# Attention's query-key products for two heads at once, on the two halves of the array's rows

## What is computed

```
# branch A, window_attention: 8 heads, 2 groups of keys (A_KV = 2), 4 heads to a group, head width 64
qg = q.reshape(B, N, Q, A_KV, A_GROUP, HEAD_DIM)
s = jnp.einsum('bnqkgd,bnskd->bnkgqs', qg, k, preferred_element_type=jnp.float32) * ATTN_SCALE
...
s = jnp.where(valid[:, None, None], s + bias, -jnp.inf)
m = jnp.maximum(jnp.max(s, axis=-1, keepdims=True), sk)
e = jnp.exp(s - m)
pr = e / (jnp.sum(e, axis=-1, keepdims=True) + jnp.exp(sk - m))
o = jnp.einsum('bnkgqs,bnskd->bnqkgd', pr.astype(v.dtype), v)
# branch B, dsa_attention: the same with keys chosen by top-k of the indexer's scores, no sink
```

## Time and profile before

| | us |
|---|---|
| runs (3) | 1043.62, 1047.68, 1048.21 |
| median | 1047.68 |
| span of the profiled execution | 1044.9 |

### The profile page before, as it was taken

The page is one execution under the profiler, slowest core; times in us unless marked ns, Lnnn a source line. Parts: engine busy times, 40 slices in busy tenths (PEclk is TensorE's granted clock), DMA queues, the critical chain, the costliest instruction groups (busy, mean ns, idle before and its releaser), DMA issues.

```text
span 1044.9 us, 14060 instructions
## 1 busy us (share of the span) xinstructions
PE 930.3 (89%) x5627; PEld 599.2 (57%) x5630; DVE 394.1 (38%) x1071; ACT 260.4 (25%) x529; POOL 123.1 (12%) x133
## 2 busy tenths in 40 slices
PE   7989998998999999998999977887987887887996
PEld 7869995456999998994333322332322222224885
DVE  4179998878242436453111101101101101101885
ACT  6254326675232323222000000000000000001541
POOL 2404730002030000001111111011010011000000
PEclk9999999999999999997999999999999999999998
DMA  8850602001925225356999999999999999996501
GB/s 262 115 153 2 201 2 61 1 1 30 299 62 158 65 61 241 127 206 249 430 425 425 426 429 427 424 429 424 427 426 427 425 427 428 425 428 250 211 26 60
DMA packets 60131, 263.71 MB, mean 252 GB/s; under 512 B 11054, under 2 KB 36030, under 8 KB 46224
## 3 DMA queue, kind: packets, MB, share of 16 engines
q1 hardware_dynamic: 54160, 250.99, 62.5%
q0 software_dynamic: 5296, 9.79, 2.6%
q10 hardware_dynamic: 624, 2.23, 0.6%
HBM read 253.99 MB, written 16.85 MB: 259 GB/s over the span
## 4 chain that ended last, share of the span: by engine, by line
PE 52%; DMA 30%; DVE 13%; ACT 2%; issue 2%; SPq 0%; DVEq 0%; ACTq 0%
DMA arena<-in_w_up 29%; PE ps L1083 13%; PE ps L1250 11%; PE ps L1115 4%; PE ps L1381 4%; DVE nrm L1901 4%; DVE hT L1905 3%; PE ps L871 3%; PE ps L1275 3%; PE ps L1365 2%; PE ps L1000 1%; PE ps L1049 1%; PE ps L1124 1%; PE ps L1028 1%; DVE xf L1905 1%
## 5 line engine op out<-in xcount | busy, mean ns | idle before, releaser
L1250 PE MATMUL ps<-arena,hT 128*64 128x512 f32 x992 | 243.7, 645 | 41.2 <-DMA arena<-in_w_up 41.0
L1250 PEld LDWEIGHTS ps<-arena,hT 128*64 128x64 f32 x992 | 74.5, 141 | 207.6 <-issue 157.5
L2185 DVE TENSOR_TENSOR xf<-xf,ps 128x256 f32<-128x256 f32 x32 | 13.5, 421 | 404.4 <-ACT xf L1666 379.0
L1083 PE MATMUL ps<-arena_merge,arena_merge 128*128 128x256 f32 x624 | 99.7, 287 | 0.0
L1275 PE MATMUL ps<-arena,xf 128*64 128x512 f32 x336 | 76.7, 598 | 12.8 <-DVE xf L2188 12.8
L1083 PEld LDWEIGHTS ps<-arena_merge,arena_merge 128*128 128x128 f32 x624 | 87.4, 188 | 0.0
L826 POOL DMA_INDIRECT expert_rows<-xf,arena x32 | 31.9, 998 | 427.0 <-ACT xf L1670 399.6
L1083 PE MATMUL ps<-xf_merge,arena_merge 128*128 128x256 f32 x480 | 82.0, 288 | 0.0
L1666 ACT ACTIVATE xf<-ps 128x256 f32<-128x256 f32 x30 | 11.5, 384 | 259.0 <-PE ps L1250 259.0
L1083 PEld LDWEIGHTS ps<-xf_merge,arena_merge 128*128 128x128 f32 x480 | 69.3, 188 | 0.0
L1670 ACT ACTIVATE xf<-ps 128x512 f32<-128x512 f32 x30 | 17.9, 597 | 159.8 <-PE ps L1275 159.8
(11 more groups left out here) (300 smaller groups left out, 1317.6 us busy)
## 6 DMA issues: line engine op xcount, KB each, us to landing
arena<-in_w_gate SPq DMA_DIRECT2D x30, 2048.0 KB, 30.0
arena<-in_w_up SPq DMA_DIRECT2D x30, 2048.0 KB, 37.5
arena<-in_w_down SPq DMA_DIRECT2D x11, 2048.0 KB, 37.3
hT<-in_w_down SPq DMA_DIRECT2D x11, 2048.0 KB, 36.5
arena<-in_w_down SPq DMA_DIRECT2D x20, 1024.0 KB, 31.5
arena<-in_w_in SPq DMA_DIRECT2D x10, 1024.0 KB, 6.4
arena<-in_w_in SPq DMA_DIRECT2D x3, 2048.0 KB, 9.9
arena<-in_w_gate SPq DMA_DIRECT2D x8, 512.0 KB, 10.2
```

The lines of the kernel that those rows point to most:

```text
L1083: mm = pe.matmul(w[:, 2 * lo_t:lo_t + hi_t], rounded(st[:, c, cols]), rounded(mv[:, c, lo_t:hi_t]), start=c == 0 and k == 0, stop=c == pla ...
L1250: mm = pe.matmul(ps[g * BLK:(g + 1) * BLK, 2 + s, :], xsT[:, c, col:col + BLK], expert_columns(k, slice(0, 2), c, g), start=c == 0, stop=c ...
```

## The change

The scores of two units of a block are now issued together, by `scores_of_two(u)` at even u. The matmul of each reads only the 64 partitions of its own group, for the queries as for the keys: one lies on the upper half of the array's rows, the other on the lower half, and they write different PSUM banks. The halves of the query planes that no matmul reads any more are not zeroed, and the semaphore that said so (`q_clean`) is gone. The wait for `max_ready` covers both banks before the first of the two.

```diff
-        pool.wait_ge(sw_split, 10)
-        for q, dst in (('qb', qb), ('qa', qx)):
-            for m in range(4):
-                pool.wait_ge(wide_full, WIDE[(q, m)].fill)
-                for h in (2 * m, 2 * m + 1):
-                    lo = (1 - h // HG) * HD
-                    link(pool.memset(dst[lo:lo + HD, plane(h), :], 0.0))
-        pool.sem_inc(q_clean, 1)
...
-        def scores(u):
+        def scores_of_two(u):
+
             br, b, j = UNITS[u]
-            if banks_before(u) is not None:
-                pe.wait_ge(max_ready, banks_before(u) + 1)
+            for v in (u, u + 1):
+                if banks_before(v) is not None:
+                    pe.wait_ge(max_ready, banks_before(v) + 1)
             if u == 0:
                 pe.wait_ge(toep_ready, 1)
-                pe.wait_ge(q_clean, 1)
...
+            two = [scores_at(u), scores_at(u + 1)]
+            last = [None, None]
             for lo in range(0, n, 512):
                 hi = min(n, lo + 512)
-                if b == 's':
-                    for hh in range(HG):
-                        mm = pe.matmul(w[32 * hh:32 * hh + NS, lo:hi], q[:, 2 * hh + j, NP:NT], kT[:, NP + lo:NP + hi],
-                                       start=True, stop=br == 'a')
-                else:
-                    k0 = P * (b + 1) - n
-                    mm = pe.matmul(w[:, lo:hi], q[:, j, tok(b)], kT[:, k0 + lo:k0 + hi], start=True, stop=br == 'a')
...
+                for hh in range(HG if b == 's' else 1):
+                    for g in range(KV):
+                        d = slice(g * HD, (g + 1) * HD)
+                        if b == 's':
+                            last[g] = pe.matmul(two[g][32 * hh:32 * hh + NS, lo:hi], q[d, 2 * hh + g, NP:NT],
+                                                kT[d, NP + lo:NP + hi], start=True, stop=br == 'a')
+                        else:
+                            k0 = P * (b + 1) - n
+                            last[g] = pe.matmul(two[g][:, lo:hi], q[d, j + g, tok(b)], kT[d, k0 + lo:k0 + hi],
+                                                start=True, stop=br == 'a')
+
+            for g in range(KV):
+                if br == 'b':
+                    m0, _ = MSK[b]
+                    for lo in range(0, n, 512):
+                        hi = min(n, lo + 512)
+                        last[g] = pe.matmul(two[g][:, lo:hi], identb[:, :], msk[:, m0 + lo:m0 + hi], start=False, stop=True)
+                last[g].then_inc(s_full, 1)
...
-        for u in range(AHEAD):
-            scores(u)
+        scores_of_two(0)
         for u in range(len(UNITS) + 3):
-            if u + AHEAD < len(UNITS):
-                scores(u + AHEAD)
+            if u % 2 == 0 and u + AHEAD < len(UNITS):
+                scores_of_two(u + AHEAD)
```

More of the change, by code:

```diff
@@ L487, in _program @@
     consts_ready = sem("consts_ready")
-    q_high, ik_high, q_clean = sem("q_high"), sem("ik_high"), sem("q_clean")
+    q_high, ik_high = sem("q_high"), sem("ik_high")
     f_high, f_split, sw_high, sw_split = (sem(n) for n in ["f_high", "f_split", "sw_high", "sw_split"])
@@ L987, in scores @@
             if br == 'b' and j == 0:
                 pe.wait_ge(masks_ready, [0, 1, 2, 3, 's'].index(b) + 1)
-            w = scores_at(u)
             n = unit_keys(br, b)
             q, kT = (qx, kaT) if br == 'a' else (qb, kbT)
+            two = [scores_at(u), scores_at(u + 1)]
+            last = [None, None]
             for lo in range(0, n, 512):
                 hi = min(n, lo + 512)
-                if b == 's':
-                    for hh in range(HG):
-                        mm = pe.matmul(w[32 * hh:32 * hh + NS, lo:hi], q[:, 2 * hh + j, NP:NT], kT[:, NP + lo:NP + hi],
-                                       start=True, stop=br == 'a')
-                else:
-                    k0 = P * (b + 1) - n
-                    mm = pe.matmul(w[:, lo:hi], q[:, j, tok(b)], kT[:, k0 + lo:k0 + hi], start=True, stop=br == 'a')
```

## The result

The change makes the kernel slower: 1049.95 us in the median of 20 runs (1043.88 to 1053.41) against 1045.05 of 20 runs of the kernel before. The ratio is 1.003, with a 95% interval of 1.0016 to 1.0043. The quotient of the two medians would be 1.0047, a little outside it; the medians of this kernel jump by some us with a few runs, and I go by the ratio. In medians that is +4.9 us where I forecast -3.0, by the ratio some +3. The time is inside my range and inside 0.5%, but the change has the other sign.

The account below looks back on a forecast made before the run. No engine is full in attention; its chain of waits sets the time, and everything behind shifts with it. Places in attention sum to -3.0 us, taking the median 1047.68 to 1044.7 us, range 1040.0 to 1050.5.

Parts of the forecast that it names:

- The sum of the places: Seven stretches of attention, estimated one by one for shorter scores, added switches and the new order: -3.0 us in all.
- The two places between 196 and 220 us: Branch a's last and b's first units (196.0 to 204.6), -1.0 us; weighing to transposes (213.4 to 219.9), -0.8 us.
- b, block 1: Branch b's block 1: three weighings on the chain, two thirds of 3 x 0.43 us saved: -0.8 us.
- b, block 0: Branch b's block 0, 128 keys: +0.2 us ahead of the weighing, -0.2 behind it: 0.
- a, blocks 1 to 3: Branch a's blocks 1 to 3: each weighing saves 0.43 us behind it, costs up to 0.35 ahead: -0.6 us.
- b's sample block: Branch b's units 50 and 51: the pair waits for row_max of unit 49 instead of 47, chain end unchanged: 0.
- the memsets at 0: Start of attention: q_clean never held PE, so removing memsets and wait is worth 0; first score within 0.2 us of 162.5.
- The clock falls: Rival in attention: two more half-clock stretches, net 0 to +0.4 us; over 0.5% slower only at four or more; chance 0.08.
- the sign of being wrong: End of attention, forecast near 254.2 us: the prediction is wrong if it comes before 251 or after 257.
- Non-overlap: Rival: row halves don't run side by side, +7 us, 1054.7; decided if a 256-key pair takes over 0.8 us; chance 0.08.
- The switches are cheaper: Rival: tiling switches cost 0.20 us a pair instead of 0.35, another -3.4 us, giving -6.4, 1041.3 us; chance 0.13.
- PE was not what the chain waited for: Rival: DVE's unchanged busy time (76.9 us) in attention makes the places give back their gains: 0, 1047.7 us; chance 0.21.

Follow-up runs that it names:

- e4: Changed kernel plus nine unused 128x128 float32 matmuls while PE waits for the start of attention; 1050.10 us, ratio 1.0031 to the kernel before.
- e7: Kernel before with row-tiled pairs only in branch b's blocks 3 and 2 (512 and 384 keys); 1045.93 us, ratio 0.9990 to the kernel before.
- e10: Kernel before with row-tiled pairs only in branch a and branch b's block 0; 1049.02 us, ratio 1.0033 to the kernel before.
- e6: Changed kernel with branch b's two sample units issued one by one on their 64 rows; 1049.46 us, ratio 1.0017 to the kernel before.
- e2: Kernel before with each score reading only its own 64 rows, one unit at a time; 1081.98 us, ratio 1.0350 to the kernel before.
- e1: Changed kernel's paired order, but each matmul over all 128 rows, memsets and q_clean back; 1048.76 us, ratio 1.0018 to the kernel before.
- e8: Kernel before with row-tiled pairs only in branch b's blocks 3, 2 and 1; 1045.20 us, ratio 0.9984 to the kernel before.
- e9: Kernel before with each prompt score split into two column halves over all 128 rows; 1049.70 us, ratio 1.0034 to the kernel before.
- e5: Kernel before plus nine unused 128x128 float32 matmuls while PE waits for the start of attention; 1046.71 us, ratio 0.9999 to the kernel before.
- e3: Changed kernel with every row-tiled score pair issued twice into the same banks; 1051.07 us, ratio 1.0043 to the kernel before.

## Why the prediction was wrong

**The sum of the places** held wherever a run shows the place at full clock. The two places between 196 and 220 us were to give -1.0 and -0.8: units 34 to 49 gain 2.0 (e4, e7) and 32 to 34 lose 0.1. "b, block 1" was -0.8: 0.7. "b, block 0" was 0: -0.3. "a, blocks 1 to 3" was -0.6: blocks 2 and 3 gain 0.5 together (e10). "b's sample block" was 0 and lies between 0 and +0.6 (e6). That makes -3.4 to -2.8 without a's blocks 0 and 1, where the forecast for all was -3.0. Those two blocks are not shown at full clock by any kernel that issues their pairs once, so their part stays open. The overlap (starts 6 ns apart), the 0.20 us on top of a pair's scores in the chain, the memsets at 0 (the first `row_max` starts between 161.5 and 163.4 us in all kernels, with and without them) and DVE's unchanged busy time were right. A pair's switches, 0.20 to 0.29 us in branch a, were less than my 0.35, which speaks for a larger gain and not for a loss.

**The step that failed is the price of the rival "The clock falls".** I let two more stretches come, at most half of each lost, and a net of 0 to +0.4 us. The profiled execution has 27.3 us more at half clock: the first fall lasts 10.2 us instead of 3.4, four more come inside attention, and one of 6.8 us at the gate. They fall where PE is what the chain waits for. Weighings cost 0.77 to 0.85 us more each, the first gate 2.3. Against -3.0 stands a net of +4.1 at the end of attention, which is the sign of being wrong that I had named (it ends at 261.3, after 257), +6.3 in all, and +4.9 in the medians. Two things were missing. I took the length of a fall from the one row before, 3.4 us. With branch a's pairs or single scores on 64 rows the first lasts 10.2, 13.7, 17.1, 17.1 and 54.6 us (changed kernel, e10, e4, e6, e2), and PE is busy for 95% of it and more; where every score of branch a runs over the whole array, it lasts 3.4 or 6.8 us (before, e1, e8, e9) or doesn't come. And I priced the fall inside attention alone. How much of the gate's 2.3 us is the change's is open, since e5 loses 2.5 there with no row tile. The condition for a loss over 0.5%, that it comes four times or more, was near: the profiled execution has four times the 6.8 us that I had priced, and its span is 0.6% longer; in the medians it is 0.5% (4.9 us), and 0.3% by the ratio.

**The other rivals.** Non-overlap is refused by the pair's 0.63 us, under the 0.8 that would have decided for it. The switches are cheaper, between the rival's 0.20 and my 0.35, but the gain of that rival didn't come. "PE was not what the chain waited for" is refused by the stretches that shrank with DVE's busy time unchanged.

**What stays open.** Order alone costs 0.18% (e1), of which the clock's part and the wait of the sample pair are parted only within bounds (in units 49 to 52, 1.7 us at most and 1.2 at least). Two accounts of the falls are not parted: each comes behind gaps on PE, and shorter scores leave more of them; and the clock stays down longer with 64 rows at work. e2 against e9 shows the second for branch a alone, and e2 and e9 differ in the form of the tiles and in the switches next to weighings too. That the form itself is not the cause rests on e3, which has the row form and full clock.

## What to carry to other kernels

In a stage where TensorE has gaps already, a change that takes matmul time out of it can cost more in granted clock than it saves: read the clock of the stage, and how long it stays down, before counting the time saved. Tile part of the products at a time, and time each part. Here the pairs paid in branch b's blocks of 256 to 512 keys and lost in branch a, whose blocks have 256 keys too, so length alone doesn't decide. Two profiles at different clocks are compared place by place, each place at the same clock, or the fall is taken for a wait.

## What the runs showed of the hardware

- Scores on 64 of the 128 rows, one after the other between transposes and weighings, kept TensorE at 1.2 GHz for 54.6 us in which it was never idle on the profile (e2, +3.5%). The same products over the whole array, in as much streaming time, left it at 2.4 GHz for all but 6.8 us (e9, +0.34%). With masks of 128 rows between them, e2's scores ran at 2.4 GHz from 219.7 to 281 us.
- Doubling row-tiled matmuls raised the grant of attention from 0.80 and 0.91 to 1.00 (e3).
- Between 162 and 270 us a fall of the clock lasted 3.4 to 17.1 us in the other kernels, and PE had gaps ahead of it each time (busy 1.2 to 2.1 of the last 3 us in the changed kernel, 1.16 in e1).
- Two float32 matmuls on two row halves, each writing all 128 partitions of a bank of its own, start 6 ns apart and take 0.63 us of the chain for 256 columns, as one over all rows does behind a switch. The Trainium skill (TensorEngine Tiling (Array Packing), Key Properties) has the change of mode drain TensorE; this trace agrees, with 0.20 us on top of the scores of each pair (0.63 against 0.43).
